# Two-expert phases of 1408 columns in place of eleven groups of 256: the expert stage of a hybrid trunk on one core

## The chip, the core and the metric

The kernel runs on one core of one Trainium2 chip. The metric is the device time of one execution in microseconds (us). One profiled execution stands beside it: its trace lists every instruction on the five engines: PE (matmul, with PEld for its weight loads), DVE (vector), ACT (scalar), POOL and SP (which issues the weight transfers).

## What is computed

A trunk of two pre-normalised residual layers over 256 frames of width 1024, in float32. The even layer is a mixer and a dense SwiGLU; the odd layer is attention and then a SwiGLU of eight experts, of which each frame uses two:

```python
def swiglu(x, w1, w3, w2):
    return (jax.nn.silu(x @ w1) * (x @ w3)) @ w2

for e in range(N_EXPERTS):   # 8
    y = y + combine[:, e:e + 1].astype(xf.dtype) * swiglu(xf, w1[e], w3[e], w2[e])
```

`w1[e]` and `w3[e]` are 1024 x 2816, `w2[e]` is 2816 x 1024: 34.6 MB of float32 weights for each expert, 277 MB for the eight. A router (256 frames x 8 logits, top two, softmax of the two) gives `combine`. One final RMSNorm ends the program.

## The kernel before

Each engine has its own program, and semaphores order them. Float32 products are made of three matmuls each (`product`, lines 280 to 283): every operand is split into a high part (`_hi`) and the rest (`_lo`), and hi x hi, hi x lo and lo x hi are summed in PSUM. The frames are the stationary operand, the weights the moving one.

**Weights.** A weight piece is 128 partitions x 2048 float32 (1 MB). SP loads it by two transfers of 512 KB into one of eleven ring buffers as soon as `lo_done` says that the buffer's last piece is split. ACT copies it to `w_hi[i % 3]` (`split_hi`, line 495; it waits for the transfer and, by `used`, for PE to have finished piece i - 3, which had the same `w_hi`), and DVE subtracts to `w_lo[i % 3]` (`split_lo`, line 1247). PE waits for `lo_done`. So PE works on one piece while at most two more are split. `SPLITS = 3` is that number of buffers.

**One expert.** PE gathers the expert's frames by a selection matrix into 128 slots (`gather`, line 1166), and adds the results back by another (`scatter`, line 1187). Between them stand 33 pieces in 11 groups g of 256 of the 2816 hidden columns. A group has two `up` pieces, each one half of K (four chunks of 128 rows) with 256 columns of w1 and 256 of w3 side by side in rows of 1 KB, and one `down` piece (256 rows of w2 in rows of 4 KB). All of it is one bank of 512 columns for a group. `ITEM` sets the order: up(0,0), up(0,1), up(1,0), up(1,1), down(0), up(2,0), up(2,1), down(1), and so on, so `down` of a group comes one group behind its `up`. When up(g,1) is done, ACT makes silu (line 633), DVE multiplies by the w3 half (line 1462); PE transposes the product (`turn`, line 1045, two of 128 x 128) after up(g+1,0), ACT and DVE split it into `hT_hi` and `hT_lo` (lines 639, 1466), and `down(g)` uses it.

ACT and DVE run the same list of pieces: at piece p they first do what belongs to it (silu or multiply, the split of the turned block) and then split piece p + 3.

```python
for p in parts:
    kind, g, half = ITEM[p]
    if kind == "up" and half == 1:
        multiply(g)
    if kind == "up" and half == 0 and g >= 1:
        turned(g - 1)
    ...
    if p + SPLITS < PER + ahead:
        split_lo(first + p + SPLITS, n)
```

Experts 0 to 7 run in a loop in their own order. Should an expert have over 128 frames, further items follow at the end; there are none here.

Of the kernel before, what the change touches and what calls it, by code (L numbers as in the profile page):

```python
# [13 lines left out]
P = 128  # L14
EPS = 1e-6

# [3 lines left out]
def trunk(nc, x, e_norm1, e_w_in, e_sgu_ln_g, e_sgu_ln_b, e_sgu_w, e_sgu_b, e_conv_w, e_a_log,  # L20
# [20 lines left out]
    SLOTS = P  # L41
# [41 lines left out]
    slots = [slot_of(i) for i in range(A_MOE + PER + SPLITS)]  # L83
# [10 lines left out]
    PER_SLOT = 32 * PER // RING  # L94

# [11 lines left out]
    with ExitStack() as ctx:  # L107
# [8 lines left out]
        ring = [sb(f"ring{i}", [P, PIECE]) for i in range(R_EVEN)]  # L116
        h = sb("h", [P, TILES, D])
        xn = sb("xn", [P, TILES, D])
        x_hi = sb("x_hi", [P, DC, SEQ], F32R)
        x_lo = sb("x_lo", [P, DC, SEQ], F32R)  # L120
        gain = sb("gain", [P, 2, D])
        ident = sb("ident", [P, P])
        ones = sb("ones", [P, P])
        neg_ones = sb("neg_ones", [P, P])
# [3 lines left out]
        neg_after = sb("neg_after", [P, P])  # L128
        level = sb("level", [P, LEVELS, P])
# [48 lines left out]
        ring += [sb(f"ring{i}", [P, PIECE]) for i in range(R_EVEN, RING)]  # L178
        w_router = sb("w_router", [P, DC, NE])
        wr_hi = sb("wr_hi", [P, DC, NE], F32R)  # L180
        wr_lo = sb("wr_lo", [P, DC, NE], F32R)
        odd = ExitStack()
# [13 lines left out]
        sel_p = sb("sel_p", [P, TILES, SLOTS])  # L196
        sel_w = sb("sel_w", [P, TILES, SLOTS])
        back = sb("back", [SLOTS, TILES, P])
        y_exp = sb("y_exp", [SLOTS, D])
        logits_T = back[0:NE, :, :].rearrange("p t n -> p (t n)")  # L200
        logits = sb("logits", [P, TILES, NE])
        rt = y_exp[:, 0:3 * TILES * NE * NE].rearrange("p (k a b) -> p k a b", k=3, a=TILES * NE)
        r2 = sb("r2", [P, 8, TILES, NE])
# [3 lines left out]
        li = spent[:, 0:24].rearrange("p (a b) -> p a b", a=3)  # L207
        item_f = spent[:, 24:48].rearrange("p (a b) -> p a b", a=3)
        li3 = spent[:, 64:128].rearrange("p (a b) -> p a b", a=8)
        table = sb("table", [P, 3, TILES, NK])  # L210
        col6 = sb("col6", [P, 3, TILES, 1])
        counts = sb("counts", [1, NE])
        item_i = sb("item_i", [1, 3, 8], I32)
# [11 lines left out]
        ring_in = [sem(f"ring_in{i}") for i in range(RING)]  # L225
# [40 lines left out]
        y_act, y_vec, scat_done, scat_added = sem("y_act"), sem("y_vec"), sem("scat_done"), sem("scat_added")  # L266
        out_ready, out_sem = sem("out_ready"), sem("out_sem")

        block = ctx.enter_context(nc.Block())

# [16 lines left out]
        def _(sp):  # L287
# [24 lines left out]
            def destination(i, p, m):  # L312
                t = ring[slots[i]]
                if ITEM[p][0] == "up":
                    return t[:, :].rearrange("p (c w n) -> p c w n", c=HC, w=2)[:, :, m, :]
                return t[:, m * D:(m + 1) * D]

            for i in range(A_MOE):
# [6 lines left out]
                if A_FFN <= i < A_QKV:  # L325
                    for m, w, rows, cs in item_sources(i - A_FFN, e_ffn_w1, e_ffn_w3, e_ffn_w2):
# [3 lines left out]
                        sp.dma_start(destination(i, i - A_FFN, m), src).then_inc(ring_in[slots[i]], 16)  # L330
# [4 lines left out]
            def load_item(n, e):  # L335
                for p in range(PER):
                    i = A_MOE + p
                    need = before_it(i) + 1 if isinstance(n, int) and n == 0 else sp.snap(n * PER + (A_MOE + p - RING + 1))
                    sp.wait_ge(lo_done, need)
                    for m, w, rows, cs in item_sources(p, o_moe_w1, o_moe_w3, o_moe_w2):  # L340
# [5 lines left out]
                        sp.dma_start(destination(i, p, m), src).then_inc(ring_in[slots[i]], 16)  # L346

            with sp.Fori(0, NE) as e:
                load_item(e, e)
            sp.wait_ge(items_ready, 1)  # L350
            n_more = sp.value_load(item_i[0:1, 0, 0:1], min_val=0, max_val=7)
            with sp.If(n_more > 0):
                with sp.Fori(0, n_more) as it:
                    e = sp.value_load(item_i[0:1, 2, bass.ds(it, 1)], min_val=0, max_val=NE - 1)
                    load_item(it + NE, e)
# [104 lines left out]
        def _(act):  # L460
# [25 lines left out]
            def split_hi(i, n=None):  # L486

                if n is None:
                    act.wait_ge(ring_in[slots[i]], arrivals(i))
                    if i >= SPLITS:  # L490
                        used(act, i - SPLITS)
                else:
                    act.wait_ge(ring_in[slots[i]], n * PER_SLOT + arrivals(i))
                    used(act, i - SPLITS, n)
                act.activation(w_hi[i % SPLITS][:, :], ring[slots[i]][:, :], ACT.Copy).then_inc(hi_done, 1)  # L495
# [212 lines left out]
            for i in range(A_MOE - 1, A_MOE + 2):  # L708
                split_hi(i)
            norm(3)  # L710
            split_hi(A_MOE + 2)
# [3 lines left out]

            def evac_y(n):
                used(act, A_MOE + PER - 1, n)
                act.activation(y_exp[:, 512:D], ps[0:SLOTS, 1, :], ACT.Copy).then_inc(y_act, 1)

            def evac_xg(k):  # L720

                for b in range(2):
                    act.wait_ge(gather_done, k * 2 + (b + 1))
# [3 lines left out]
            def expert(n, ahead, parts):  # L727
                def before_end():
                    if ahead:
                        evac_xg(n + 1)  # L730
                    evac_y(n)
                ffn(1, A_MOE, TILES * FG, FG, ahead, n, parts, {PER - 1: before_end})

            evac_xg(0)
            expert(0, SPLITS, HEAD)
            with act.Fori(0, NE - 1) as n:
                expert(n, SPLITS, REST)
                expert(n + 1, SPLITS, HEAD)
            expert(NE - 1, 0, REST)
            act.wait_ge(items_ready, 1)  # L740
            n_more = act.value_load(item_i[0:1, 0, 0:1], min_val=0, max_val=7)
            with act.If(n_more > 0):
                with act.Fori(0, n_more) as it:
                    for p in range(SPLITS):
                        split_hi(A_MOE + p, it + NE)
                    evac_xg(it + NE)
                    expert(it + NE, 0, ALL_PARTS)
# [5 lines left out]
        def _(pe):  # L753
# [257 lines left out]
            def ffn(tiles, first, unit0, group0, x, n=None, between=None, parts=ALL_PARTS, fresh=None):  # L1011
# [3 lines left out]
                def up(g, half):  # L1015

                    i = first + at_up(g, half)
                    if n is not None and g == 0:
                        pe.wait_ge(xgl_ready, n * 2 + (half + 1))
# [15 lines left out]
                def turn(g):  # L1035

                    pe.wait_ge(act_ready, count(n, FG, unit0 + tiles * (g + 1)))
                    if n is not None and g == 0:
                        pe.wait_ge(back_ready, n + 1)
# [118 lines left out]
            def gather(k):  # L1158

                pe.wait_ge(prep_done, k * 4 + 2)  # L1160
                if not isinstance(k, int):
# [545 lines left out]
```

## Time and profile before

| | us |
|---|---|
| device time, median of 3 runs (1393.3 to 1397.37) | 1393.67 |
| profiled execution, first to last instruction (span) | 1392.7 |
| PE busy in the span (96%) | 1340.7 |
| PE weight loads (80%) | 1108.7 |
| DVE busy (73%) | 1011.5 |
| ACT busy (59%) | 819.1 |
| from the first gather (560.8) to the end of the span | 831.9 |

The profiled execution's own time is not listed apart from its span; the span is 1.0 us under the median of the runs. Weight loads overlap matmuls. The page's share of busy time is a mean over the whole span: the even layer and the attention take the first 560 us and the expert stage, which the change rewrites, the rest. A matmul's record is longer than the distance to the next, since matmuls are pipelined; distances are read from the starts.

### The profile page before, as it was taken

The numbers are of one execution on the slowest core, as the hardware profiler recorded it, in microseconds if no ns is written. First come the engines' busy times: TensorE is split into PE (matmuls) and PEld (weight loads), VectorE is DVE, ScalarE is ACT, GpSimd is POOL, SyncE is SP. The second block draws the span as 40 slices with busy tenths as digits, with TensorE's granted clock in tenths as the row PEclk, the third lists the DMA queues.
The fourth block names the chain that finished last, engine by engine and source line by source line (L and its number), as shares of the span: only waits on it lengthen the run. The fifth ranks groups of instructions, "written<-read, shape, count | busy, mean of one in ns | idle before, by whom it ended". The sixth has DMA issues, their size and how long they took to land.

```text
span 1392.7 us, 19384 instructions
## 1 busy us (share of the span) xinstructions
PE 1340.7 (96%) x6803; PEld 1108.7 (80%) x6803; DVE 1011.5 (73%) x922; ACT 819.1 (59%) x789; POOL 52.7 (4%) x89
## 2 busy tenths in 40 slices
PE   5999899999989998999999999999999999999996
PEld 5899778888879986788788788788788788787884
DVE  3965454444454464788888888888988988888885
ACT  4752253333344573577677676677677676676674
POOL 7000000000000150000000000000000000000000
PEclk9999689999999999999999999999999999999999
DMA  9521329555535413599899899899899999999970
GB/s 311 163 91 41 110 85 366 185 186 188 185 123 182 152 31 106 192 364 365 290 366 363 288 369 361 288 366 363 292 363 345 308 364 333 320 364 331 322 250 32
DMA packets 267173, 351.72 MB, mean 253 GB/s; under 512 B 10913, under 2 KB 238257, under 8 KB 267121
## 3 DMA queue, kind: packets, MB, share of 16 engines
q1 hardware_dynamic: 265824, 347.12, 73.1%
q0 software_dynamic: 1296, 3.90, 1.0%
q8 instruction: 34, 0.56, 0.2%
q14 instruction: 19, 0.15, 0.0%
HBM read 349.93 MB, written 1.05 MB: 252 GB/s over the span
## 4 chain that ended last, share of the span: by engine, by line
PE 92%; DVE 2%; ACT 2%; POOL 2%; issue 1%; DMA 1%; DVEq 0%; POOLq 0%; ACTq 0%
PE ps L281 26%; PE ps L282 26%; PE ps L283 26%; PE ps L1166 2%; PE ps L1187 2%; PE ps L1045 2%; PE ps L1092 1%; PE ps L938 1%; POOL level L372 1%; PE ps L1102 1%; DMA gam<-in_e_sgu_w_dram 1%; PE ps L914 1%; PE ps L933 1%; ACT xn L475 0%; PE ps L978 0%
## 5 line engine op out<-in xcount | busy, mean ns | idle before, releaser
L1247 DVE TENSOR_TENSOR w_lo<-ring,w_hi 128x2048 fp32r<-128x2048 f32 x329 | 754.1, 2292 | 208.5 <-ACT w_hi L495 207.5
L495 ACT ACTIVATE w_hi<-ring 128x2048 fp32r<-128x2048 f32 x329 | 630.1, 1915 | 96.5 <-PE ps L283 92.3
L281 PE MATMUL ps<-w_hi,x_hi 128*128 128x512 f32 (+1 forms) x1040 | 412.2, 396 | 2.2 <-ACT xn L582 1.7
L282 PE MATMUL ps<-w_lo,x_hi 128*128 128x512 f32 (+1 forms) x1040 | 401.6, 386 | 0.0
L283 PE MATMUL ps<-w_hi,x_lo 128*128 128x512 f32 (+1 forms) x1040 | 401.3, 386 | 0.0
L283 PEld LDWEIGHTS ps<-w_hi,x_lo 128*128 128x128 f32 x1040 | 196.6, 189 | 43.4
L281 PEld LDWEIGHTS ps<-w_hi,x_hi 128*128 128x128 f32 x1040 | 196.7, 189 | 42.5 <-ACT xn L582 1.9
L282 PEld LDWEIGHTS ps<-w_lo,x_hi 128*128 128x128 f32 x1040 | 196.8, 189 | 38.1 <-issue 0.2
L281 PE MATMUL ps<-w_hi,hT_hi 128*128 128x512 f32 x440 | 174.4, 396 | 2.7 <-DVE hT_lo L1466 2.5
L282 PE MATMUL ps<-w_lo,hT_hi 128*128 128x512 f32 x440 | 174.1, 396 | 0.0
L283 PE MATMUL ps<-w_hi,hT_lo 128*128 128x512 f32 x440 | 173.8, 395 | 0.0
L639 ACT ACTIVATE hT_hi<-ps 128x256 fp32r<-128x256 f32 (+1 forms) x99 | 40.4, 408 | 163.4 <-PE ps L1045 163.4
L281 PEld LDWEIGHTS ps<-w_hi,hT_hi 128*128 128x128 f32 x440 | 82.5, 188 | 22.9 <-issue 2.9
L283 PEld LDWEIGHTS ps<-w_hi,hT_lo 128*128 128x128 f32 x440 | 82.6, 188 | 19.8
L633 ACT ACTIVATE silu_s<-ps 128x256 f32<-128x256 f32 x110 | 41.0, 383 | 97.2 <-PE ps L283 97.2
L282 PEld LDWEIGHTS ps<-w_lo,hT_hi 128*128 128x128 f32 x440 | 82.5, 188 | 19.5
L281 PE MATMUL ps<-x_hi,w_hi 128*128 128x256 f32 x288 | 84.2, 292 | 4.2 <-DVE x_lo L1241 4.2
L283 PE MATMUL ps<-x_hi,w_lo 128*128 128x256 f32 x288 | 83.0, 288 | 0.0
L282 PE MATMUL ps<-x_lo,w_hi 128*128 128x256 f32 x288 | 82.8, 288 | 0.0
L1466 DVE TENSOR_TENSOR hT_lo<-ps,hT_hi 128x256 fp32r<-128x256 f32 (+1 forms) x99 | 44.4, 448 | 26.5 <-ACT hT_hi L639 26.5
L281 PEld LDWEIGHTS ps<-x_hi,w_hi 128*128 128x128 f32 x288 | 56.3, 196 | 5.3 <-DVE w_lo L1247 4.4
L282 PEld LDWEIGHTS ps<-x_lo,w_hi 128*128 128x128 f32 x288 | 56.2, 195 | 0.2 <-issue 0.2
(297 smaller groups left out, 961.4 us busy)
## 6 DMA issues: line engine op xcount, KB each, us to landing
ring<-in_o_moe_w_dram SPq DMA_DIRECT2D x528, 512.0 KB, 4.8
ring<-in_e_ffn_w_dram SPq DMA_DIRECT2D x66, 512.0 KB, 4.9
ring<-in_e_w_in_dram SPq DMA_DIRECT2D x24, 512.0 KB, 8.8
ring<-in_o_w_qkv_dram SPq DMA_DIRECT2D x24, 512.0 KB, 4.4
ring<-in_e_w_out_dram SPq DMA_DIRECT2D x8, 512.0 KB, 4.3
ring<-in_o_w_out_dram SPq DMA_DIRECT2D x8, 512.0 KB, 4.2
h<-in_x_dram SPq DMA_DIRECT2D x2, 512.0 KB, 4.1
gain<-in_e_norm_dram POOLq DMA_DIRECT2D x2, 512.0 KB, 5.2
```

The costliest lines, as they stand in the source:

```text
L281: pe.matmul(o, a_hi, b_hi, start=first, stop=False)
L282: pe.matmul(o, a_hi, b_lo, start=False, stop=False)
L283: return pe.matmul(o, a_lo, b_hi, start=False, stop=last)
L372: after(pool.affine_select(out=t, in_=t, pattern=pattern, compare_op=op, fill=fill, base=base, channel_multiplier=cm))
L495: act.activation(w_hi[i % SPLITS][:, :], ring[slots[i]][:, :], ACT.Copy).then_inc(hi_done, 1)
L633: act.activation(silu_s[:, t, :], ps[:, bank, 0:CW], ACT.Silu).then_inc(silu_done, 1)
L639: act.activation(hT_hi[:, g % 2, :, 0:tiles * P], ps[:, 7 if tiles == 2 else 3, 0:2 * tiles * P].rearrange("p (j n) -> p j n", j=2), ACT.C ...
L1045: last = pe.transpose(ps[:, t_bank, at:at + P], h_act[:, g % 2, t, j * P:(j + 1) * P], ident[:, :])
L1166: last = mm(ps[:, 6 + c // 4, at:at + SLOTS], xn[:, t, c * P:(c + 1) * P], sel_p[:, t, :], start=(t == 0), stop=(t == TILES - 1))
L1187: mm(ps[:, SCAT_BANKS[m], :], back[:, t, :], y_exp[:, hf * 512:(hf + 1) * 512], start=True, stop=True)\
L1247: tt(w_lo[i % SPLITS][:, :], ring[slots[i]][:, :], w_hi[i % SPLITS][:, :].bitcast(F32), ALU.subtract).then_inc(lo_done, 1)
L1466: tt(hT_lo[:, g % 2, :, 0:tiles * P], ps[:, 7 if tiles == 2 else 3, 0:2 * tiles * P].rearrange("p (j n) -> p j n", j=2), hT_hi[:, g % 2, : ...
```

## The change

Every line outside the expert stage computes the same as before. In the expert stage:

- **Phases.** The 2816 hidden columns of an expert are cut in two halves of 1408 (`HALF`), so there are 16 phases n (expert q, half a). `WORK` is the order: up 0, up 1, down 0, up 2, down 1, up 3, ..., down 14, down 15.
- **up** has 16 steps: for each of the eight K chunks one of w1 and one of w3, each a weight piece of 128 x 1408. A step is three products into three banks (512, 512 and 384 columns), so the sums over K of w1 fill banks 0 to 2 and those of w3 banks 3 to 5 while K runs outermost.
- **down** has six steps: five of two 128-row blocks of w2 (128 x 2048) and one of one block (128 x 1024), summed in banks 6 and 7 over both halves.
- **Between them.** silu and the product run once a phase over 512, 512 and 384 columns, and the eleven transposes (`turn_up`) stand before the second step of the next `down`; they write banks 0 to 2. Gather, scatter and the way back stand before later steps of `down` ("hooks").
- **Transfers.** One for each step instead of two for each piece: 720,896 bytes in rows of 5.6 KB for w1 and w3, 1 MB in rows of 4 KB for w2. They are laid end to end in the same bytes as the eleven ring buffers (`place_pieces`), and 18 semaphores count arrivals.
- **Order of the experts.** `rank_experts` sorts experts 1 to 7 by their number of frames, on DVE inside the first phase; `list_items` moves there too. `big(q)` is True for all eight, so every expert keeps 128 slots and the three matmuls of a product; the branches for small experts are never taken.
- `SPLITS` stays 3. The stage is written out, not looped.

The core of the diff:

```diff
+    def big(q):
+        return True
+    PHASE = [(q, a) for q in range(NE) for a in range(2 if big(q) else 1)]
+    WORK = [("up", 0), ("up", 1)]
+    for n in range(2, PHASES):
+        WORK += [("down", n - 2), ("up", n)]
+    WORK += [("down", PHASES - 2), ("down", PHASES - 1)]
...
+            def split_step_hi(v):
+                st, i = STEPS[v], A_MOE + STEPS[v].at
+                act.wait_ge(ring_in[arrive_sem(v)], arrive_count(v))
+                used(act, i - SPLITS)
+                act.activation(w_hi[i % SPLITS][:, 0:st.size], in_ring(WHERE[v][0], st.size), ACT.Copy).then_inc(hi_done, 1)
...
+            def silu_up(n):
+                stepped(act, last_step("up", n))
+                if n:
+                    act.wait_ge(hT_done, TURN0 + PARTS * n)
+                for b, (c0, w) in enumerate(UP_COLS):
+                    act.activation(u_act[:, c0:c0 + w], ps[:, b, 0:w], ACT.Silu).then_inc(silu_done, 1)
...
+            def turn_up(n, parts=range(PARTS)):
+                pe.wait_ge(act_ready, ACT0 + PARTS * (n + 1))
+                for b in parts:
...
+                    for i, j in enumerate(turn_blocks(b)):
+                        last = pe.transpose(ps[:, turn_bank(n, b), i * P:(i + 1) * P], u_act[:, j * P:(j + 1) * P], ident[:, :])
+                    last.then_inc(hT_done, 1)
...
+            def up_step(v, st):
...
+                    for b, (c0, n) in enumerate(UP_COLS):
+                        last = product(pe, ps[:, o + b, 0:n], xg_hi[:, c, :], xg_lo[:, c, :], hi[:, c0:c0 + n], lo[:, c0:c0 + n],
+                                       c == 0, c == DC - 1)
+                    last.then_inc(piece_used, 1)
...
+            def before_up(st):
...
+                    if n == 1:
+                        turn_up(0, (0, 1))
+                        return
+                    pe.wait_ge(xgl_ready, 2 * (q + 1))
+                    pe.wait_ge(hTl_ready, TURN0 + PARTS * n)
...
+                    turned = sum(LAST[k] <= n - 2 for k in range(NE))
+                    if turned:
+                        pe.wait_ge(back_ready, turned)
...
+            def before_down(st):
...
+                    if st.hook == 1:
+                        turn_up(after)
+                    if st.hook == 2 and LAST[q] == after and q + 1 < NE:
+                        gather(q + 1)
...
+                    if st.hook == 3:
+                        scatter(PHASE[n - 1][0], (0, 1))
+                    if st.hook == 4:
+                        scatter(PHASE[n - 1][0], (2, 3))
+                if st.hook == 5 and LAST[st.q] == n:
+                    way_back(st.q)
...
+            def gate_up(n):
+                for b, (c0, w) in enumerate(UP_COLS):
+                    vec.wait_ge(silu_done, ACT0 + PARTS * n + b + 1)
+                    tt(u_act[:, c0:c0 + w], u_act[:, c0:c0 + w], ps[:, 3 + b, 0:w], ALU.mult).then_inc(act_ready, 1)
...
+            for v, st in enumerate(STEPS):
...
+                if st.kind == "down":
+                    n, following = st.n, st.n + 1
+                    if following < PHASES:
+                        q = PHASE[following][0]
+                        if st.hook == 0:
+                            gate_up(following)
+                        if st.hook == 1:
+                            turned_lo(following)
...
+                    if st.hook == 5 and LAST[st.q] == n:
+                        back_out(st.q)
+                        if st.q + 1 < NE:
+                            places_gated(st.q + 1, tab)
+                if v + SPLITS < len(STEPS) and STEPS[v + SPLITS].big:
+                    split_step_lo(v + SPLITS)
```

In DVE's program after the change, around a `down` phase (w_lo is the split, `arena_a` and `arena_c` are the ring's bytes, u_act the product of silu and w3, m_lo the turned block):

```order
L1658 TENSOR_TENSOR w_lo<-arena_a,w_hi 128x1408 [waits hi_done] x5
L1658 TENSOR_TENSOR w_lo<-arena_a,w_hi 128x2048 [waits hi_done]
L1658 TENSOR_TENSOR w_lo<-arena_c,w_hi 128x2048 [waits hi_done] x2
L2063 TENSOR_TENSOR u_act<-u_act,ps 128x512 [waits silu_done] x2
L2063 TENSOR_TENSOR u_act<-u_act,ps 128x384 [waits silu_done]
L1658 TENSOR_TENSOR w_lo<-arena_c,w_hi 128x2048 [waits hi_done]
L2073 TENSOR_TENSOR m_lo_59<-ps,m_hi_57 128x512 [waits hTh_ready] x2
L2073 TENSOR_TENSOR m_lo_59<-ps,m_hi_57 128x384 [waits hTh_ready]
L1658 TENSOR_TENSOR w_lo<-arena_c,w_hi 128x2048 [waits hi_done]
L1658 TENSOR_TENSOR w_lo<-arena_c,w_hi 128x1024 [waits hi_done]
L1658 TENSOR_TENSOR w_lo<-arena_c,w_hi 128x1408 [waits hi_done] x2
L2081 COPY back<-ps 128x256 [waits back_done]
```

Three splits of `down` pieces stand ahead of the product of the phase before (line 2063). The third of them can start only when PE has finished the last `up` step, whose `w_hi` it takes.

In PE's program after the change, from the last matmuls of an `up` phase into `down` (m_hi and m_lo are the turned block):

```order
L462 MATMUL ps<-w_hi,xg_hi 128x384
L463 MATMUL ps<-w_lo,xg_hi 128x384
L464 MATMUL ps<-w_hi,xg_lo 128x384
L462 MATMUL ps<-w_hi,m_hi_57 128x512 [waits y_vec,lo_done,y_act,hTl_ready]
L463 MATMUL ps<-w_lo,m_hi_57 128x512
L464 MATMUL ps<-w_hi,m_lo_59 128x512
...
L1445 MATMUL ps<-ident,u_act 128x128 [waits act_ready]
L1445 MATMUL ps<-ident,u_act 128x128 x10
L462 MATMUL ps<-w_hi,m_hi_57 128x512 [waits lo_done]
```

Twelve matmuls of 512 columns, one step of `down`, stand between the end of `up` and the transposes.

In PE's program before the change, the same way for a group of 256 columns:

```order
L283 MATMUL ps<-w_hi,hT_lo 128x512
L1020 REGISTER_ALU
L281 MATMUL ps<-w_hi,x_hi 128x512 [waits act_ready,lo_done]
...
L283 MATMUL ps<-w_hi,x_lo 128x512
L1037 REGISTER_ALU
L1045 MATMUL ps<-ident,h_act 128x128 [waits hTl_ready,act_ready]
L1045 MATMUL ps<-ident,h_act 128x128
```

There a `down` piece and an `up` piece, 24 matmuls, stand between the end of up(g,1) and the two transposes.

## Rows read from the trace of the kernel before

**Rows 1.** The page's head: the span of the profiled execution.

```profile
span 1392.7 us, 19384 instructions
```

**Rows 2.** Chain of waits from 590 us: start us, us, engine, tile, line, count.

```profile
659.27 3.57 PE ps L1166 x32
...
671.26 3.59 PE ps L1187 x8
...
761.49 3.57 PE ps L1166 x32
```

**Rows 3.** Waits, 590 to 1350 us: total us, times, longest.

```profile
ACT w_hi L495 <- PE ps L283: 40.1, 76, 0.7
```

**Rows 4.** Timeline of PE, 808 to 815 us: start us, us, instruction.

```profile
808.57 0.39 PE L283 MATMUL ps<-w_hi,x_lo 128*128 128x512 f32 x1
...
811.36 0.39 PE L283 MATMUL ps<-w_hi,hT_lo 128*128 128x512 f32 x1
...
814.40 0.38 PE L1045 MATMUL ps<-ident,h_act 128*128 128x128 f32 x2
```

**Rows 5.** Stretches: length, busy of PE, PEld, DVE, ACT, POOL, clock, DMA share, GB/s.

```profile
196.00:200.00 4.00, 3.79 (x17) 2.71 (x15) 3.75 (x4) 0.32 (x2) 0.00 (x0) 1.00 0.00 0
...
590.00:1350.00 760.00, 760.00 (x3418) 606.71 (x3417) 661.04 (x506) 529.41 (x432) 0.00 (x0) 1.00 0.98 339
...
802.90:811.50 8.60, 8.60 (x40) 6.92 (x39) 7.52 (x6) 6.32 (x5) 0.00 (x0) 1.00 1.04 366
```

**Rows 6.** Timeline of PE at 197 us.

```profile
197.05 0.39 PE L282 MATMUL ps<-w_lo,x_hi 128*128 128x512 f32 x1
...
197.29 0.39 PE L283 MATMUL ps<-w_hi,x_lo 128*128 128x512 f32 x1
```

**Rows 7.** Timeline of PE at 411 us: matmuls of 256 columns.

```profile
411.04 0.28 PE L282 MATMUL ps<-x_lo,w_hi 128*128 128x256 f32 x1
...
411.16 0.28 PE L283 MATMUL ps<-x_hi,w_lo 128*128 128x256 f32 x1
```

**Rows 8.** Groups by line and shape, 590 to 1350 us: busy us, mean ns.

```profile
L1247 DVE TENSOR_TENSOR w_lo<-ring,w_hi 128x2048 fp32r<-128x2048 f32 x247 | 566.3, 2293 | 93.9 <-ACT w_hi L495 93.0
...
L495 ACT ACTIVATE w_hi<-ring 128x2048 fp32r<-128x2048 f32 x247 | 473.1, 1915 | 40.1 <-PE ps L283 40.1
...
L1462 DVE TENSOR_TENSOR h_act<-silu_s,ps 128x256 f32<-128x256 f32 x82 | 34.0, 414 | 0.0
...
L1638 DVE TENSOR_TENSOR h<-h,ps 128x512 f32<-128x512 f32 x28 | 17.9, 682 | 0.2
...
L724 ACT ACTIVATE x_hi<-ps 128x512 fp32r<-128x512 f32 x14 | 8.3, 594 | 6.3 <-PE ps L1166 6.3
```

**Rows 9.** Timeline of ACT, then of DVE, 803 to 812 us.

```profile
803.17 1.93 ACT L495 ACTIVATE w_hi<-ring 128x2048 fp32r<-128x2048 f32 x1 [0.53 <-PE ps L283]
...
811.79 1.92 ACT L495 ACTIVATE w_hi<-ring 128x2048 fp32r<-128x2048 f32 x1 [0.52 <-PE ps L283]
...
805.13 2.29 DVE L1247 TENSOR_TENSOR w_lo<-ring,w_hi 128x2048 fp32r<-128x2048 f32 x1 [0.16 <-ACT w_hi L495]
...
807.34 0.42 DVE L1466 TENSOR_TENSOR hT_lo<-ps,hT_hi 128x256 fp32r<-128x256 f32 x1
```

**Rows 10.** Groups by line, 800 to 1300 us: a small DVE instruction.

```profile
L1602 DVE TENSOR_TENSOR r<-r 1x64 f32<-1x64 f32 x1 | 0.2, 215 | 0.0
```

**Rows 11.** Timeline of PE: transposes after two waits.

```profile
203.01 3.67 PE L764 MATMUL ps<-ident,xn 128*128 128x128 f32 x16 [3.22 <-DVE xn L1233]
...
548.07 1.09 PE L764 MATMUL ps<-ident,xn 128*128 128x128 f32 x8 [3.11 <-DVE xn L1233]
```

**Rows 12.** Stretches around three idle times of PE, columns as in Rows 5.

```profile
200.00:209.00 9.00, 5.76 (x21) 5.02 (x22) 6.61 (x9) 8.19 (x14) 1.45 (x2) 0.62 0.95 328
...
402.00:410.00 8.00, 6.90 (x34) 6.29 (x35) 6.01 (x7) 4.40 (x8) 0.00 (x0) 0.59 0.01 2
...
544.00:552.00 8.00, 3.61 (x25) 2.52 (x24) 6.03 (x9) 5.12 (x13) 0.00 (x0) 1.00 0.42 131
```

More of the change, by code:

```diff
@@ L1 @@
 import math
+from collections import namedtuple
 from contextlib import ExitStack
@@ L15 @@
 EPS = 1e-6
+Step = namedtuple("Step", "kind n q a j hook part size big at ends")
 EXP_LN = "natural_log_exp_and_others"
@@ L81, in slot_of @@
         return i % R_EVEN if i < A_FFN else (i - A_FFN + 1) % RING
-    slots = [slot_of(i) for i in range(A_MOE + PER + SPLITS)]
+    slots = [slot_of(i) for i in range(A_MOE)]
     def before_it(i):
@@ new lines, in trunk @@
+        assert end[0] <= gain_at
+        put, end = over(odd_at)
+        m_hi = [put(f"m_hi{k}", [P, HB, P], F32R) for k in range(2)]
+        m_lo = [put(f"m_lo{k}", [P, HB, P], F32R) for k in range(2)]
+        assert end[0] <= nc.sbuf_usable_end
+        m_raw = [over(odd_at + 4 * HALF * k)[0](f"m_raw{k}", [P, HB, P]) for k in range(2)]
+        put, end = over(masks_at)
+        logits = put("logits", [P, TILES, NE])
+        r2 = put("r2", [P, 8, TILES, NE])
+        nat = put("nat", [P, 8, NE])
@@ new lines, in scatter @@
+            def scatter(q, parts=range(4)):
+                pe.wait_ge(hTl_ready, TURN0 + PARTS * min(LAST[q] + 3, PHASES))
+                pe.wait_ge(back_ready, q + 1)
+                pe.wait_ge(y_act, q + 1)
+                pe.wait_ge(y_vec, q + 1)
+                for m in parts:
+                    t, hf = m // 2, m % 2
+                    if big(q):
+                        a, y = back[:, t, :], y_exp[:, hf * 512:(hf + 1) * 512]
+                    else:
+                        rows = slice(hf * SMALL, (hf + 1) * SMALL)
+                        a, y = back[rows, t, :], y_exp[rows, 0:512]
+                    mm(ps[:, MOE_SCAT[m], :], a, y, start=True, stop=True).then_inc(scat_done, 1)
@@ new lines, in _, with gather_item @@
+            gather(0)
+            pe.wait_ge(counts_read, 1)
+            for v, st in enumerate(STEPS):
+                if st.kind == "up":
+                    before_up(st)
+                    up_step(v, st)
+                else:
+                    before_down(st)
+                    down_step(v, st)
+            pe.wait_ge(scat_added, 4 * (NE - 1))
+            scatter(NE - 1)
+            def gather_item(k):
+                pe.wait_ge(prep_done, k * 2 + 2 * (NE + 1))
+                pe.wait_ge(xgl_ready, k * 2 + 2 * NE)
```

626 lines of the change are left out of this document (475 added, 151 removed).

## The prediction

> **What bounds the kernel now.** I read the head of the page [rows 1], then the chain of waits in the expert stage, which is what the change rewrites. Gather follows gather (659.27 and 761.49) after 102.22 us [rows 2], once an expert, and the chain between them is PE alone. The list of waits from 590 to 1350 us has no row for PE and none for a transfer; ACT waits 40.1 us for PE to give back `w_hi` [rows 3]. So PE sets the pace, without a gap. Its work adds up: twelve matmuls of 512 columns take 811.36 - 808.57 = 2.79 us [rows 4], 0.233 each; an expert has 33 pieces x 12 = 396, so 92.3 us; gather and scatter take 3.6 each [rows 2]; the remaining 2.7 are 24 transposes at 0.11. That is 102.2. The transfers look like a second bound: from 590 to 1350 us DMA is 0.98 busy at 339 GB/s while PE is full [rows 5]. But with no transfer at all (0 GB/s from 196 to 200 [rows 5]) two matmuls stand 0.24 us apart [rows 6], the same distance, and nothing waits for a transfer.
>
> **PE's own work does not shrink.** An expert after the change has 288 up matmuls (192 of 512 columns, 96 of 384) and 132 of down: 202,752 columns, exactly 396 x 512. The 24 more weight loads stay hidden, since matmuls of 256 columns follow each other at 0.12 us [rows 7], half of 0.233, so 384 columns should take 0.175. Gather, scatter, 22 transposes and the way back are as before. PE's floor stays 102.2 us an expert, and ACT and DVE, which lose some instructions (11 small silu, products and splits become 6 larger ones) and win 11 more weight splits, were covered. Larger rows and fewer transfers: 0, since nothing waited for a transfer. The change can therefore only add waits of PE. All of them follow from one number that it leaves alone: three `w_hi`/`w_lo` buffers.
>
> Prices, from [rows 8]: a split of 2048 columns is 1.92 us on ACT and 2.29 on DVE; by the 512-column rows (0.59 and 0.68) a piece of 1408 is 1.36 on ACT and 1.62 on DVE, and a DVE operation of 384 between 0.41 and 0.68, 0.55. ACT starts 0.04 us after PE's record ends (811.36 + 0.39, then 811.79), DVE 0.03 after ACT (803.17 + 1.93, then 805.13), and DVE's next starts 0.08 before the last ends (805.13 + 2.29, then 807.34) [rows 4, 9]. A record of PE ends 0.16 after the next matmul could start.
>
> **Wait A, at the transposes, 15 times.** Let t = 0 be the end of the last `up` step. Only now may ACT copy the third `down` piece: ends 1.96; DVE's split of it ends 4.28. DVE's program has the product of silu and w3 behind that split, so the three products start at 4.20, 4.80 and 5.40 and end at 5.95; silu on ACT (three of about 0.6 behind 1.96) is done by 3.8 and hidden. PE may transpose at 6.0. Meanwhile it had one `down` step, 12 x 0.233 = 2.80, so it is free at 2.64. PE waits 3.4 us; 15 x 3.4 = 51. Before, the same way had 24 matmuls, 5.8 us from 808.57 to 814.40 [rows 4], and a chain with one small product. Behind the waiting transposes stands everything else on PE; ACT waits for them with the splits that follow, but PE has two split pieces in hand then. Bounds: 2.8 if the products overlap more, 4.0 if ACT comes later.
>
> **Wait A0, once.** Between up 0 and up 1 no `down` step covers the way, and the piece is 1408: ACT to 1.40, DVE to 3.05, products to 4.75, PE free at -0.16: 5.0 us.
>
> **Wait B, the first `down` piece, 15 times.** Its split starts when the third last `up` step ends: 0.04 + 1.92 + 0.03 + 2.29 + 0.05 = 4.3. PE has two steps of 1408 x 3 columns, 2 x 1.92 less 0.16 = 3.7. It waits 0.6: 9 us. In the steady `up` steps 1.36 + 1.62 + 0.12 = 3.1 is less than 3.7, so there is no wait; in `down` 4.3 is less than 5.4.
>
> **Wait C, the way back, 7 times.** The `up` after an expert's last `down` waits for `back_ready`. DVE copies `back` behind the split of a 1408 piece whose `w_hi` came free at the end of the fifth step: 0.04 + 1.36 + 0.03 + 1.62 - 0.08 + 0.42 + 0.05 = 3.4. PE has two transposes and six matmuls, 1.6 less 0.16. It waits 2.0: 14 us.
>
> **The first expert.** Ranking the experts and listing the items put about 35 small instructions on DVE inside up 0, at 0.2 us [rows 10] some 7 to 9 us. DVE has 1.92 - 1.54 = 0.38 to spare a step, 6 in the phase, but not where the work stands. Between 0 (all absorbed) and 9 (nothing absorbed); I take 4. At the start and end of the stage a few table copies and a turn go: -1.
>
> Waits: 51 + 5 + 9 + 14 + 4 - 1 = **82 us**. On the profiled execution: 1392.7 + 82 = 1474.7; on the median, 1.0 above, 1475.7.
>
> **The clock.** PE idle is dearer than its length. After an idle of 3.2 us [rows 11] the granted clock over 200 to 209 was 0.62 on average [rows 12], that is 9 x 0.38 / 0.5 = 6.8 us at 1.2 GHz; sixteen transposes took 3.67 where eight at 2.4 GHz took 1.09 [rows 11], 1.5 more. From 402 to 410 it was 0.59: 6.6 us. But after an idle of 3.1 us, 545 to 548, it stayed 1.00 [rows 11, 12]. So a wait of 3.4 us may or may not halve the clock. A fall costs between 1.5 (the transposes alone) and 3.4 (half of 6.8); some of its time falls in the idle itself or at waits B and C, so I take 2.0, nearer the lower row, and two falls in three waits as in these three places: 11 x 2.0 = **22 us**. Bounds: 0 and 16 x 3.4 = 54. The page "TensorE: Matmul & The Clock Gate" of the Trainium skill, section "HAM oscillation — how this bites in real kernels", speaks against this change: a wait in each round of a loop can throttle PE in every round, at half the throttled time. By it all sixteen would fall, 16 x 3.4, and the sum would be 1530; the trace, with one of three that did not fall, agrees in kind and not in number.
>
> **Forecast: 1475.7 + 22 = 1497.7, so 1498 us,** 7.5% slower.
>
> **The rivals.** *Waits without the clock*: the falls do not come, as at 545 us; 1476 us. For it: the idle is near the one that did not fall. *Every wait falls and costs full*: 1475.7 + 54 = 1530. For it: the way is the same each time; against it the row at 545 us. *Transfers were the bound* (the other side): if transfers in rows of 1 KB at 339 GB/s pace the stage, 277 MB take 817 us, as near to 8 x 102.2 as PE's sum. At the 366 GB/s that a stretch of two groups reaches [rows 5] larger rows would take 757, 60 less; PE, which on this reading has slack, would take the waits A to C in it, and the time would be 1334. It decides only if part of PE's 0.233 is a hidden wait for data: 512 columns at 2.4 GHz are 0.213, and those 9% would have to go. Against it: the same distance with 0 GB/s [rows 5, 6]. The Trainium skill, "DMA: Bandwidth & Descriptors", section "Rules for kernel authors", has 1 MiB and more a transfer for best bandwidth, which this change nearly reaches; by that rule the transfers get faster, and nothing in the trace turns that into time. *The change shows nothing*: if the engines ran far enough ahead that A to C vanish, PE's floor is what is left, 1393. Against it: `used(i - 3)` ties ACT to PE.
>
> **How the numbers follow.** Forecast (waits and some falls, 1480 to 1520): 0.62. Waits alone, 1465 to 1480: 0.15. All fall, 1520 to 1535: 0.13. Transfers were the bound: 0.03. Nothing shows: 0.03. Beyond 1535, by waits that feed each other: 0.04. The range that holds 8 in 10 runs from 1468 (waits A at their lower bound of 2.8 would save 9, with no first-expert term saved and few falls) to 1530. A measurement of this kernel can tell about 0.3% from no change. Faster by more: 0.04 (the transfers, and a little of the fourth rival); within: 0.02; slower: 0.94.
>
> **What would show it.** In the new profile: transposes (line 1445) with an idle of 3.4 us before their first, 15 times, ended by DVE's product (line 2063), 5.0 once; PE's waits of 0.6 for w_lo and 2.0 for `back`; an expert period of 112 us and more instead of 102.2; a granted clock of 0.5 in a few us behind about two of three such waits; matmuls of 512 columns still 0.233 apart and of 384 0.175; no engine waiting for a transfer. The prediction is wrong if transposes start without idle, if matmul distances change, or if ACT waits for transfers.

## The result, and the profile after

| | before | after |
|---|---|---|
| device time, median, us | 1393.49 (1392.93 to 1397.37) | 1501.42 (1483.81 to 1509.81, 4 runs) |
| ratio, 95% interval | | 1.0731 [1.0669, 1.0793] |
| profiled execution, span, us | 1392.7 | 1499.3 |
| granted clock, mean of the span | 0.979 | 0.963 |
| from the first gather to the end, us | 831.9 | 939.1 |

(The kernel before was timed again beside the changed one.) The changed kernel takes 1501 us, where 1498 was forecast; by the ratio it is 7.3% slower. The ratio and its interval compare fast runs alone, so they leave out the run of 1510 us, which counts as slow; the two medians by themselves would give 7.7%. The four runs differ by 26 us, and their mean clock goes with it: 0.977 in the run of 1484 us, 0.953 in that of 1510.

A word on the title: each expert is worked in two phases of 1408 hidden columns. No phase holds two experts.

The page's head and, further down, its DMA line, of the changed kernel. Against [rows 1]: 107 us more.

```profile
span 1499.3 us, 17594 instructions
...
PE 1371.2 (91%) x6995; PEld 1154.1 (77%) x6995; DVE 1014.6 (68%) x938; ACT 835.4 (56%) x797; POOL 52.5 (4%) x89
...
DMA packets 116935, 352.19 MB, mean 235 GB/s; under 512 B 8096, under 2 KB 55216, under 8 KB 116848
```

The change does what it says: the same bytes in 116,935 packets where there were 267,173. PE's share of the span fell from 96 to 91%, and no engine waits for a transfer. What is new stands in the list of PE's waits (total us, times, longest) from 555 us to the end:

```profile
PE ps L1445 <- DVE u_act L2063: 48.9, 16, 4.8
PE ps L462 <- DVE back L2081: 14.8, 7, 2.1
PE ps L462 <- DVE w_lo L1658: 13.8, 18, 1.9
```

These are the waits A with A0 (the transposes), C (the way back) and B (the first `down` piece). Of the 18 in the third row 15 are waits B; two, of 1.91 and 1.93 us, lie in the first expert (575 and 585 us) and one, of 0.19, in the last `down` (1472 us). Before, between 590 and 1350 us, there was none [rows 3].

The chain of waits (start, us, what) through one wait A and the gathers at both ends of an expert, whose distance was 102.22 us in [rows 2]:

```profile
651.04 3.57 PE ps L1433 x32
...
748.56 1.93 ACT w_hi L713
...
750.51 6.70 DVE w_lo L1658 x3
757.21 1.67 DVE u_act L2063 x3
758.88 0.04 issue
758.92 1.42 PE ps L1445 x11
763.14 3.57 PE ps L1433 x32
...
878.33 3.57 PE ps L1433 x32
997.85 3.57 PE ps L1433 x32
```

Expert follows expert after 112.1, 115.2 and 119.5 us. Twice an expert the path leaves PE for 10 us: ACT copies a piece, DVE makes three splits one behind the other, then the three products, and only then may PE transpose. PE has work for most of these 10 us; it idles in waits B and A.

The timeline of PE around the same place (start, us, instruction, in brackets its idle time and what ended it), with two distances between matmuls of 384 columns ahead of it and, behind it, the transposes and two matmuls at 871 us:

```profile
740.09 0.34 PE L462 MATMUL ps<-w_hi,xg_hi 128*128 128x384 f32 x1
740.27 0.34 PE L463 MATMUL ps<-w_lo,xg_hi 128*128 128x384 f32 x1
740.44 0.34 PE L464 MATMUL ps<-w_hi,xg_lo 128*128 128x384 f32 x1
...
752.95 0.47 PE L462 MATMUL ps<-w_hi,m_hi 128*128 128x512 f32 x1 [0.65 <-DVE w_lo L1658]
753.26 0.40 PE L463 MATMUL ps<-w_lo,m_hi 128*128 128x512 f32 x1
...
755.36 0.40 PE L463 MATMUL ps<-w_lo,m_hi 128*128 128x512 f32 x1
755.59 0.39 PE L464 MATMUL ps<-w_hi,m_lo 128*128 128x512 f32 x1
758.92 1.42 PE L1445 MATMUL ps<-ident,u_act 128*128 128x128 f32 x11 [2.94 <-DVE u_act L2063]
...
871.37 2.61 PE L1445 MATMUL ps<-ident,u_act 128*128 128x128 f32 x11 [2.94 <-DVE u_act L2063]
...
874.20 0.63 PE L463 MATMUL ps<-w_lo,m_hi 128*128 128x512 f32 x1
874.62 0.63 PE L464 MATMUL ps<-w_hi,m_lo 128*128 128x512 f32 x1
```

The columns cost what the forecast said: 384 in 0.175 us, 512 in 0.23. The bracket understates a wait. It counts from the end of the last record, which is 0.16 us after PE could have gone on (755.59 + 0.23 against 755.59 + 0.39), so each wait A costs 3.10, each B 0.81 and each C 2.27 us. The same eleven transposes take 1.42 us here and 2.61 at 871 us, and the matmuls of 512 columns behind them stand 0.42 to 0.43 us apart, not 0.23: that is the clock.

Stretches of the changed kernel (length, busy PE, PEld, DVE, ACT, POOL, granted clock, DMA share, GB/s):

```profile
869.00:878.00 9.00, 6.63 (x23) 5.74 (x24) 6.18 (x8) 3.12 (x4) 0.00 (x0) 0.62 1.02 399
...
719.00:725.00 6.00, 5.21 (x17) 4.44 (x18) 3.42 (x7) 2.01 (x3) 0.00 (x0) 0.72 0.77 266
...
1169.00:1175.00 6.00, 6.00 (x32) 5.09 (x33) 3.74 (x4) 3.22 (x4) 0.00 (x0) 1.00 1.01 409
```

Read in stretches of 3 us from 600 to 1400 us, the granted clock goes down to its lower level, 1.2 GHz, in eleven stretches: eight start at a wait A or A0 (602, 701, 869, 929, 989, 1049, 1220, 1283 us), and three at the way back (719, 950, 1070). Behind the other waits, of the same length, it stayed at 2.4 GHz, as at 1169.

**The sum.** Waits A 15 x 3.10 = 46.5, A0 5.0, B 15 x 0.81 = 12.2, C 7 x 2.27 = 15.9, the two waits for w_lo in the first expert 4.2 and the one in the last `down` 0.3: 84.1 us. The stage grew by 939.1 - 831.9 = 107.2. That leaves 23.1 us, or 2.1 for each of the eleven stretches of low clock, if they are all of it. They are nearly all: an estimate from the distances between PE's instructions in the eleven stretches, against the same shapes at 2.4 GHz, gives 21 to 22 us, between 0.9 and 2.5 a stretch. Most of the rest is in the first matmul behind a wait B or C, which stands 0.31 us from the next (752.95, 753.26) instead of 0.23: 22 x 0.08 = 1.8.

### The profile page after: what moved, and what is told of

It reads as the page before. It is cut to its first block, busy times and chain, and to the rows that moved or that the text cites. A ratio compares the mean times of both kernels' runs of the same rounds, so it can differ in the third digit from the quotient of the medians.

```text
span 1499.3 us, 17594 instructions
## 1 busy us (share of the span) xinstructions
PE 1371.2 (91%) x6995; PEld 1154.1 (77%) x6995; DVE 1014.6 (68%) x938; ACT 835.4 (56%) x797; POOL 52.5 (4%) x89
## 2 busy tenths in 40 slices
DMA packets 116935, 352.19 MB, mean 235 GB/s; under 512 B 8096, under 2 KB 55216, under 8 KB 116848
## 4 chain that ended last, share of the span: by engine, by line
PE 80%; DVE 12%; ACT 4%; POOL 2%; issue 1%; DMA 1%; POOLq 0%; ACTq 0%; DVEq 0%
PE ps L462 22%; PE ps L463 22%; PE ps L464 22%; DVE w_lo L1658 8%; ACT w_hi L713 3%; PE ps L1445 2%; PE ps L1433 2%; PE ps L1469 2%; DVE u_act L2063 2%; PE ps L1360 1%; PE ps L1206 1%; POOL level L581 1%; PE ps L1370 1%; DMA gam<-in_e_sgu_w_dram 1%; PE ps L1182 0%
## 5 line engine op out<-in xcount | busy, mean ns | idle before, releaser
L1658 DVE TENSOR_TENSOR w_lo<-arena_c,w_hi 128x1408 fp32r<-128x1408 f32 (+2 forms) x192 | 339.4, 1778 | 121.6 <-ACT w_hi L713 121.6
L713 ACT ACTIVATE w_hi<-arena_c 128x1408 fp32r<-128x1408 f32 (+2 forms) x192 | 289.8, 1510 | 168.2 <-PE ps L464 168.2
L1658 DVE TENSOR_TENSOR w_lo<-arena_a,w_hi 128x1408 fp32r<-128x1408 f32 (+2 forms) x160 | 275.8, 1732 | 90.2 <-ACT w_hi L713 90.2
L462 PE MATMUL ps<-w_hi,xg_hi 128*128 128x512 f32 (+1 forms) x768 | 293.9, 383 | 18.6 <-DVE back L2081 14.8
L713 ACT ACTIVATE w_hi<-arena_a 128x1408 fp32r<-128x1408 f32 (+2 forms) x160 | 235.2, 1470 | 134.2 <-PE ps L464 134.2
L463 PE MATMUL ps<-w_lo,xg_hi 128*128 128x512 f32 (+1 forms) x768 | 291.5, 380 | 0.0
L464 PE MATMUL ps<-w_hi,xg_lo 128*128 128x512 f32 (+1 forms) x768 | 290.3, 378 | 0.0
L462 PE MATMUL ps<-w_hi,x_hi 128*128 128x512 f32 (+1 forms) x336 | 125.7, 374 | 1.9 <-ACT xn L800 1.7
L463 PE MATMUL ps<-w_lo,x_hi 128*128 128x512 f32 (+1 forms) x336 | 123.0, 366 | 0.0
L464 PE MATMUL ps<-w_hi,x_lo 128*128 128x512 f32 (+1 forms) x336 | 122.9, 366 | 0.0
```

The lines of the kernel that those rows point to most:

```text
L462: pe.matmul(o, a_hi, b_hi, start=first, stop=False)
L463: pe.matmul(o, a_hi, b_lo, start=False, stop=False)
L464: return pe.matmul(o, a_lo, b_hi, start=False, stop=last)
L713: act.activation(w_hi[i % SPLITS][:, 0:st.size], in_ring(WHERE[v][0], st.size), ACT.Copy).then_inc(hi_done, 1)
L1658: tt(w_lo[i % SPLITS][:, 0:st.size], in_ring(WHERE[v][0], st.size), w_hi[i % SPLITS][:, 0:st.size].bitcast(F32), ALU.subtract).then_inc(lo ...
```

## The experiments

Eight kernels in two groups (e3, e1, e6 and e2; then e7 to e10), each group timed beside the kernel before on the same chip (before: 1393.53 us for the first group, 1394.09 for the second). Each is an edit of the changed kernel, unless it says of another one.

| | median, us (range) | ratio to before, 95% interval |
|---|---|---|
| changed kernel | 1501.42 (1483.81 to 1509.81) | 1.0731 [1.0669, 1.0793] |
| e3, PE busy in waits A | 1477.75 (1476.27 to 1480.23) | 1.0597 [1.0569, 1.0624] |
| e1, product ahead of the third split | 1449.04 (1447.56 to 1451.85) | 1.0392 [1.0364, 1.0419] |
| e6, transposes a step later | 1444.78 (1442.17 to 1446.32) | 1.0359 [1.0332, 1.0387] |
| e2, way back earlier | 1480.02 (1479.08 to 1481.46) | 1.0612 [1.0586, 1.0637] |
| e7, e1 + e2 + e6 | 1414.88 (1413.74 to 1418.22) | 1.0151 [1.0137, 1.0164] |
| e8, e7 in rows of 1.4 and 1 KB | 1415.34 (1414.12 to 1416.71) | 1.0155 [1.0142, 1.0169] |
| e9, e7 + first `down` piece in halves | 1404.39 (1403.95 to 1408.19) | 1.0085 [1.0070, 1.0100] |
| e10, e9 + the first expert's waits | 1397.35 (1395.12 to 1399.68) | 1.0028 [1.0016, 1.0040] |

### e3: the wait kept, PE's idle filled

```diff
                     if st.hook == 1:
+                        for _k in range(13):
+                            pe.matmul(ps[:, 6, :], zero[:, :], m_hi[n % 2][:, 0:4, :].rearrange("p a b -> p (a b)"), start=False, stop=False)
                         turn_up(after)
```

Thirteen matmuls with a stationary operand of zeros run in each of the 15 waits A and add nothing to the sums. This takes the clock apart from the wait.

> Thirteen matmuls of 512 columns with an all-zero stationary block are put on PE ahead of the transposes in the 15 down phases, summed into bank 6, to which they add 0. They take 13 x 0.233 = 3.0 us, the length of wait A (2.94 us by the records), so PE is busy while DVE's chain runs and the transposes start when they did. Theory (the waits of PE cost twice, once by their length and once by the clock that falls behind them): the waits in time stay, the falls in the 15 phases go; the granted clock behind the first expert is 1.00, and the time is about 23 us below the changed kernel's 1501, so 1478 (1473 to 1485), still some 84 above the kernel before; what is left of falls is the one behind the 5-us wait between up 0 and up 1. Rival (the clock follows the mean load, not the idle times, or the 23 us come from elsewhere): no change, 1490 to 1510. Rival (the filler delays the transposes): slower, over 1505.

Measured: 1477.75 us, where 1478 was expected: 23.7 us less than the changed kernel, by adding work to PE. PE's waits in e3:

```profile
PE ps L464 <- DVE back L2085: 14.9, 7, 2.2
PE ps L464 <- DVE w_lo L1662: 13.8, 18, 1.9
PE ps L1447 <- DVE u_act L2067: 4.9, 1, 4.9
```

A stretch of 830 us in e3, columns as above:

```profile
640.00:1470.00 830.00, 802.01 (x3734) 656.55 (x3732) 649.71 (x497) 531.99 (x434) 0.00 (x0) 1.00 0.80 295
```

The same stretch of the changed kernel:

```profile
640.00:1470.00 830.00, 761.34 (x3471) 626.26 (x3470) 637.36 (x488) 525.05 (x427) 0.00 (x0) 0.97 0.81 295
```

Waits B and C are there unchanged and the idle of A is gone; the clock is 1.00 for 830 us. The rival by which the waits alone make the time falls: the clock cost some 24 us (21.3 in the profiled executions from the first gather on; the stretch behind A0 stays in e3 too). That is against the median of the changed kernel. Its fastest run, 1483.81 us at a mean clock of 0.977, is only 6 us above e3, whose four runs had 0.978 to 0.983: where the clock was high by itself, the filler had little left to save.

### e1 and e6: wait A taken apart in two ways

e1 puts silu and the product at the end of the last `up` step, ahead of the third split in ACT's and DVE's programs:

```diff
-                    if st.hook == 0:
-                        gate_up(following)
...
+                if st.kind == "up" and st.ends:
+                    gate_up(st.n)
                 if v + SPLITS < len(STEPS) and STEPS[v + SPLITS].big:
                     split_step_lo(v + SPLITS)
```

> silu on ACT and the product on DVE stand ahead of the split of the third down piece and no longer behind it; PE's program is the same. Theory (wait A is DVE's order): silu can start when up ends, the products when DVE has finished the split of the second down piece, about 2.3 us after up, so they end at 4.2 and wait A is about 1.2 to 1.6 in place of 3.1: 15 x 1.7 = 25 to 30 us less, 2 less at the 5-us wait; an idle of under 2 us lets the clock stand: 20 more. 1501 - 50 = 1451 (1440 to 1462). Rival (the third split, now later, stops PE at the third down step): wait B or a new wait for w_lo grows by what A loses, and the time stays over 1480.

e6 leaves that order and moves the transposes, and what ACT and DVE make of them, behind one more `down` step (hook 2 for hook 1, on the three engines):

```diff
-                    if st.hook == 1:
+                    if st.hook == 2:
                         turn_up(after)
```

> The eleven transposes stand before the third step of down and not before the second, on PE, ACT and DVE; nothing else moves. DVE's chain (third split, then the three products) ends 6.0 us after up as before, and PE now has two down steps, 24 matmuls and 5.6 us less 0.16, in front of the transposes. Theory: wait A falls from 3.1 to about 0.6 in 15 phases, 37 us less, and with no idle of 3 us the clock does not fall there, 20 us less: 1501 - 57 = 1444 (1438 to 1455). Waits B, C and that of 5 us stay. Rival (ACT or DVE as a whole are too slow in a down phase, 12 + 4 to 7 us of DVE work in 15 to 20, and the transposes' place does not matter): the waits turn up one step later, for the splits, and the time stays over 1485.

Measured: e1 1449.04 us, e6 1444.78, each within 2 us of what was expected. PE's waits in e1, then in e6:

```profile
PE ps L1444 <- DVE u_act L2062: 14.0, 16, 2.9
```

```profile
PE ps L1445 <- DVE u_act L2063: 5.0, 2, 4.8
```

The chain of waits of e1, through one of its waits A, has two splits ahead of the product, not three:

```profile
794.36 4.50 DVE w_lo L1657 x2
798.86 1.67 DVE u_act L2062 x3
800.53 0.04 issue
800.57 1.42 PE ps L1444 x11
```

So the third split in DVE's program is the cause of most of wait A (e1 keeps PE's order, and of the 2.94 us a phase 2.2 are gone), and one more `down` step, 2.8 us, is as good a cover (e6). Of the 56.6 us that e6 saves, 46.5 are the waits, less some 2 for a new one (a scatter waits once, 1.9, for the turned block); some 12 are clock. That is half of the 24 of e3. So e6's time was met partly by luck: its expectation had 37 us of waits and 20 of clock. Between 640 and 1400 us the clock still falls four times in e6 and five times in e1, now at the way back (e6: 710, 926, 1034 and 1250 us), though in e3, with the same seven idle times of 2.1 us there, it never does.

### e2: the way back two steps earlier

```diff
-                if st.hook == 5 and LAST[st.q] == n:
+                if st.hook == 3 and LAST[st.q] == n:
                     way_back(st.q)
```

> The two transposes of the way back, DVE's copy of them and the next gated selection stand at the fourth step of an expert's last down, not at the sixth. Theory: wait C (seven times, 2.1 us by the records) disappears, and nothing else changes: 14 to 16 us less, 1486, the clock's falls as before; since the falls alone move the changed kernel's runs between 1484 and 1510, the wait's row in the trace is the surer sign. Rival (up would wait for something else that is late at the same time, the last split or bank 6 and 7): the wait for back goes and one for w_lo of the same length comes, 1495 to 1505.

Measured: 1480.02 us, 21.4 less than the changed kernel and 6 under what was expected. The wait for `back` is gone from the list and the others are what they were:

```profile
PE ps L1445 <- DVE u_act L2063: 49.0, 16, 4.8
PE ps L462 <- DVE w_lo L1658: 13.8, 18, 1.9
```

The waits C are 15.9 of the 21.4. In the profiled executions, from the first gather to the end, e2 is 939.1 - 921.0 = 18.1 us shorter, so some 2 us are clock there; the other 3 are within what the changed kernel's own runs differ by. The falls of the clock did not become fewer, as one might think from the changed kernel, where three stand at the way back. Read in stretches of 3 us, e2 has eleven as well, all at the transposes: at A0 and at ten of the 15 waits A, where the changed kernel had seven. (At 752 us, for one, the clock is 0.50 over 752 to 758, and the eleven transposes take 2.61 us.) The expectation, the clock's falls as before, holds for their number and not for their places.

### e7: the three moves together

> Silu and the product ahead of the split of the third down piece, the transposes one down step later, and the way back at the fourth down step instead of the sixth. If the waits add up as read: the u_act waits of the down phases (15 x 3.1) go and with them the clock's 23 us, the waits for the way back (7 x 2.1 + 0.16 = 16) go, the one wait between up 0 and up 1 shrinks from 5.0 to about 3. What stays is 12 us at the first down piece, 4.5 in the first expert and 3: 1393.5 + 12 + 4.5 + 3 - 1 = 1412 us, with a granted clock of 1.00 behind the first expert. Rival, that larger row transfers or the new order of the work cost PE something that no wait shows: 1425 or more with the same list of waits.

Measured: 1414.88 us, 3 over what was expected. The three effects add up. PE's waits in e7:

```profile
PE ps L462 <- DVE w_lo L1657: 13.8, 18, 1.9
PE ps L1444 <- DVE u_act L2062: 2.9, 1, 2.9
...
PE ps L1468 <- DVE m_lo L2072: 2.2, 1, 2.2
```

A stretch of 660 us in e7:

```profile
640.00:1300.00 660.00, 652.23 (x3090) 540.74 (x3091) 560.98 (x431) 459.69 (x376) 0.00 (x0) 1.00 0.89 333
```

Most of the 3 us is one wait that the expectation had left out: a scatter (line 1468) that stands behind the later transposes waits once, 2.2 us, for the split of the turned block. The trace of e6 had it already, with 1.9.

### e8: does the length of a row matter?

```diff
+                if st.kind == "up":
+                    for k in range(4):
+                        cs = slice(k * (st.size // 4), (k + 1) * (st.size // 4))
+                        sp.dma_start(dst[:, cs], src[:, cs]).then_inc(ring_in[arrive_sem(v)], 16)
```

and the same for w2 in quarters of 256 columns; the counts of arrivals follow.

> As e7, but each step's weights come by four transfers of a quarter of the columns each: rows of 1408 bytes for w1 and w3 and of 1 KB for w2, in place of 5.6 and 4 KB. If PE sets the pace and no transfer is late, this is the time of e7 within 0.3%. Rival (the transfers were near to being the bound, so that the longer rows are what keeps it away): with the rows of before the transfers take 8 x 102 us again at 339 GB/s and any stall adds, so e8 is slower than e7 by 1% or more and ACT shows waits for transfers.

Measured: 1415.34 us against 1414.88, 0.03% apart, with overlapping intervals. The same stretch as in e7:

```profile
640.00:1300.00 660.00, 652.23 (x3091) 540.73 (x3091) 560.58 (x432) 459.10 (x375) 0.00 (x0) 1.00 0.99 334
```

The transfers are 0.99 busy instead of 0.89 for nearly the same rate (334 and 333 GB/s), in 299,739 packets instead of 116,935, and the time is the same. The long rows take 10% of the transfers' busy time away; PE never waited for it. The rival by which the transfers were the bound falls. (Two things change at once in e8, the length of a row and the number of transfers. As the sum of both shows nothing, that does no harm here; but the rows of w2 are shorter than the 4 KB of the kernel before, so e8 is the harder case and not a copy of it.)

### e9: wait B

```diff
+                m = st.size // 2 if st.kind == "down" and st.hook == 0 else 0
+                if m:
+                    vec.wait_ge(half_done, st.n + 1)
+                    tt(w_lo[i % SPLITS][:, 0:m], in_ring(WHERE[v][0], st.size)[:, 0:m], w_hi[i % SPLITS][:, 0:m].bitcast(F32),
+                       ALU.subtract)
                 vec.wait_ge(hi_done, i + 1)
```

> As e7, and the first down piece of a phase is copied and split in two halves of 1024 columns, so that DVE starts when ACT has done half. ACT and DVE then need 0.04 + 1.0 + 0.03 + 1.2 + 1.2 = 3.5 in place of 4.3 us, under the 3.7 that PE has for two up steps: the waits of 0.8 at the first down piece (15 times, 12 us) go. 1400 us. Rival, that this wait is not ACT and DVE in a row but DVE late from earlier work: then the halves change nothing and it stays at 1412.

Measured: 1404.39 us, 10.5 less than e7 where 12 were expected. Of PE's 18 waits for w_lo the 15 at the first `down` piece are gone; the two of the first expert and the short one in the last `down` are left:

```profile
PE ps L463 <- DVE w_lo L1666: 4.0, 3, 1.9
```

So wait B is ACT and DVE in a row on one piece, 4.3 us by the prediction's prices against PE's 3.7. The trace has none of the 15 left, which by 15 x 0.81 is 12.2 us; 1.7 of them are not in the time. The wait for the turned block (2.2 us in e7) is 2.7 here, and the granted clock falls behind it, which it did not in e7. The chain of waits of e9, four matmuls of the scatter behind that wait and four that follow:

```profile
1360.42 3.49 PE ps L1472 x4
1366.70 1.72 PE ps L1472 x4
```

The clock is 0.57 over 1360 to 1364 us, and the first four take 1.8 us longer. With the 0.5 of the wait that is 2.3, in one profiled execution.

### e10: the first expert

```diff
+                        if st.n == 1 and st.j < 2:
+                            pe.wait_ge(act_ready if w else silu_done, ACT0 + b + 1)
...
-                        turn_up(0, (0, 1))
...
+                if n == 1 and st.j == 2:
+                    turn_up(0, (0, 1))
```

and on DVE the ranking and the list of items come two small instructions to a step, the list only in up 2.

> As e9, and two places in the first expert: up 1 starts on each bank as silu or the product of up 0 has read it, with the transposes of up 0 two steps later (the wait of about 3 goes), and the ranking and the list of items run two small DVE instructions to a step in place of up to 20 at once (the 4.5 us go). If PE's own work is what it was before the change (102.2 us an expert), nothing is left to wait for and the time is that of the kernel before within 0.5%: 1395 us, 1390 to 1400. Rival, that the new shape costs PE something by itself (more weight loads, 384 columns): it stays above 1400 with no waits left.

Measured: 1397.35 us, 1.0028 [1.0016, 1.0040] of the kernel before, 7.0 less than e9. PE's waits in e10:

```profile
PE ps L1472 <- DVE m_lo L2108: 2.7, 1, 2.7
...
PE ps L463 <- ACT u_act L957: 0.8, 1, 0.8
...
PE ps L463 <- DVE w_lo L1669: 0.2, 1, 0.2
```

and its chain, gather to gather:

```profile
733.17 3.57 PE ps L1436 x32
...
835.47 3.57 PE ps L1436 x32
...
937.82 3.57 PE ps L1436 x32
```

An expert takes 102.30 and 102.35 us, against 102.22 in [rows 2]. With its waits gone the changed kernel has the pace of the kernel before: PE's own work in the new shape is the same to 0.1 us an expert. What remains is 3.3 us by the medians and 837.4 - 831.9 = 5.5 by the profiled executions from the first gather on. Most of it is the one wait for the turned block, 2.7, and the clock, which falls behind it as in e9 (0.62 over 1352 to 1356 us).

## Why the prediction was right

| term | predicted | in the trace | by experiment |
|---|---|---|---|
| PE's own work, an expert | 102.2 | | 102.3 (e10) |
| rows and transfers | 0 | no engine waits for one | 0.5, within the scatter (e8 against e7) |
| wait A, 15 times | 51 | 46.5 | 56.6 with its clock (e6) |
| wait A0, once | 5.0 | 5.0 | |
| wait B, 15 times | 9 | 12.2 | 10.5 (e9) |
| wait C, 7 times | 14 | 15.9 | 21.4 with its clock (e2) |
| first expert | 4 | 4.2, and 0.3 in the last `down` | 7.0 with the 3.1 of A0 that e9 still had, and the clock behind it (e10) |
| clock | 22 | 23.1 | 23.7 (e3) |

- **The floor.** The prediction took PE's sum of columns as the bound and held that nothing waits for the transfers, 0.98 busy as they are. e10 and e8 show both.
- **Wait A: the size was nearly right, the way to it was not.** The prediction let DVE begin the third split when ACT's copy, started at the last `up` step's end, was done, and reached the transposes 6.0 us after that end. The chain shows that DVE was not waiting for ACT there: it came straight from the second split, three in a row, 6.70 us, behind a copy (748.56) that PE had released at the end of the third last `up` step. Counted from the same end (752.95 - 0.65 = 752.30), the transposes came at 6.6. But PE too began its covering `down` step later, by wait B, which the prediction had costed and not carried on. The two offset each other: 3.1 us for 3.4, which is luck. The prediction also laid all waits to the three `w_hi`/`w_lo` buffers. For wait A that holds for the piece that starts the chain, at 748.56, and not for the third, on which it laid it; no run had a fourth buffer, so what one would save isn't shown.
- **Waits B and C** were 0.2 to 0.3 us a time longer than forecast: B 0.81 for 0.6, C 2.27 for 2.0. For B it is the hand-overs: ACT started 0.10 us after PE's record (748.12 + 0.34, then 748.56) and PE 0.15 after DVE's (750.51 + 2.29, then 752.95), where 0.04 and 0.05 were taken.
- **The clock.** Eleven falls at 2.0 us were forecast; eleven stretches at 2.1 are in the trace. The count is partly luck. It is that of one profiled execution near the median, and by the times and clocks of the single runs the term was far smaller at 1484 us than at 1510. The forecast had all of them at the transposes, two in three. Eight were there, one in two, and three behind the way back, where the forecast had idle times of 2.0 us and no fall. The upper bound of 3.4 us a fall took half of the time at 1.2 GHz as lost; 512 columns take 0.42 to 0.43 us there (874.20 to 874.62) and 0.233 at 2.4 GHz, so 45% is lost, and part of the low stretch passes while PE idles anyway. In prediction and trace alike an idle of 3 us sometimes brings the lower clock and sometimes not ([rows 11, 12] before; 871 and 1169 us after). The Trainium skill, "TensorE: Matmul & The Clock Gate", section "HAM oscillation — how this bites in real kernels", lets a wait in each round throttle each round. The trace agrees in kind and not in number: 11 of the 23 waits of over 2 us at the transposes and the way back were followed by the lower clock. The kernel on that page waits longer in each round than waits A to C do, so the two don't contradict each other.
- **The spread.** The range was 1468 to 1530. The four runs of the changed kernel used 26 us of it by themselves, and their time goes with their mean clock. e2, whose clock falls too, spread over 2.4 us only, so four runs don't tell how wide that is.

What stays open: why, of waits of one length at one place in the program, some bring the lower clock and others don't. Three of seven did at the way back in the changed kernel, five in e1, four in e6, none in e3. Of the 15 waits A seven did in the changed kernel and ten in e2. Whether work taken from PE, in gather or scatter, would bring e10 under the kernel before wasn't tried.

## What to carry to other kernels

When one engine is full and the transfers beside it look full too, look first at whether any engine waits for a transfer. None did here, and longer rows bought nothing; what decided was what the new tiling did to the order of small work behind large work. List, for each engine's program, what stands ahead of each hand-over (here one split of 2.2 us ahead of a product), and give PE as much work there as that takes: three moves in the order and one piece in halves won back 97 of 108 us, and two places in the first expert 7 more. If a wait must stay, a few matmuls by zeros in it can be worth their while, because PE's idle time may cost the clock behind it as well.

## What was unexpected of the hardware

- The granted clock fell to 1.2 GHz behind an idle of 2.1 us: 0.72 over 719 to 725 us. [Rows 11] showed it after 3.2 us. The trace of the kernel before had shorter ones as well, and the forecast could have read it there: the low stretch from 402 to 410 us in [rows 12] stands behind idle times of 2.57 and 0.77 us:

```profile
402.10 1.09 PE L764 MATMUL ps<-ident,xn 128*128 128x128 f32 x8 [2.57 <-DVE xn L1233]
403.97 1.97 PE L764 MATMUL ps<-ident,xn 128*128 128x128 f32 x8 [0.77 <-DVE xn L1233]
```

- Work of no use can shorten the time: e3 gives PE 15 x 13 matmuls more and is 23.7 us faster by the medians, with every other wait as it was.
- The idle time in brackets is 0.16 us shorter than what a wait costs, since a matmul's record runs past the moment at which the next could start. Over the 41 waits of PE that the list shows at these three places that is 6.6 us of 107.
